# A weight ring filled by halves: two transfers for each pair of weight chunks

## The reference

```python
for l in range(2):                      # first model
    proj = rmsnorm(x) @ w_in            # 1024 x 9x1024 and more
    y = gates * (ssd(...) @ w_ssd_out, mla(...) @ w_mla_out, gdn(...) @ w_gdn_out)
    h = x + sum(y) @ w_out
    x = h + square(relu(rmsnorm(h) @ w_up)) @ w_down
x = rmsnorm(x) * final_gain
for i in range(2):                      # second model, with a context of 256 more tokens
    mods = silu(c, c_ctx) @ ada_w[i] + ada_b[i]
    x = x + g1 * mixer(modulated(x))    # neighbourhood attention, then a gated scan
    x = x + g2 * (silu(a) * u) @ ffn_w_out[i]   # a, u = modulated(x) @ ffn_w_in[i]
```

## Time and profile before

| | |
|---|---|
| Median of 3 runs | 2593.07 us (2590.92 to 2595.86) |
| Span of the profiled execution, first to last instruction | 2594.1 us |
| TensorE busy | 2512.4 us (97%), 19246 matmuls |
| VectorE, ScalarE, GpSimd busy | 1460.9, 1250.7, 312.5 us |
| Moved by the weight queue | 375.90 MB, 41.6% of 16 DMA engines' time |
| Ring transfers | 1024 KB each, 4.8 us from issue to landing (median) |

### The profile page before, as it was taken

The page is one execution under the profiler, slowest core; times in us unless marked ns, Lnnn a source line. Parts: engine busy times, 40 slices in busy tenths (PEclk is TensorE's granted clock), DMA queues, the critical chain, the costliest instruction groups (busy, mean ns, idle before and its releaser), DMA issues.

```text
span 2594.1 us, 44101 instructions
## 1 busy us (share of the span) xinstructions
PE 2512.4 (97%) x19246; PEld 2321.4 (89%) x19246; DVE 1460.9 (56%) x2242; ACT 1250.7 (48%) x1838; POOL 312.5 (12%) x179
## 2 busy tenths in 40 slices
PE   7999999999999999999999999999999999998999
PEld 7989998999999999979999886787779998888999
DVE  4773775665457557746665248553334554676554
ACT  6645554454366365445554267542223443335442
POOL 5113000000151120000000005200000001331000
PEclk9999999999999999999999999999999999999999
DMA  4344444455543443435554335233334542113454
GB/s 171 133 143 161 147 149 145 171 185 182 181 147 131 146 159 134 166 128 195 179 189 142 108 116 210 82 116 144 130 130 173 201 162 95 68 50 130 163 189 169
DMA packets 56018, 383.90 MB, mean 148 GB/s; under 512 B 6033, under 2 KB 9745, under 8 KB 10001
## 3 DMA queue, kind: packets, MB, share of 16 engines
q1 hardware_dynamic: 55104, 375.90, 41.6%
q10 hardware_dynamic: 720, 5.18, 0.5%
HBM read 380.01 MB, written 1.05 MB: 147 GB/s over the span
## 4 chain that ended last, share of the span: by engine, by line
PE 82%; DVE 9%; ACT 5%; DMA 2%; issue 1%; POOL 0%; DVEq 0%; POOLq 0%; ACTq 0%
PE ps L915 21%; PE ps L916 20%; PE ps L917 20%; DVE r L2112 3%; PE ps L1042 1%; PE ps L1420 1%; ACT r L1478 1%; PE ps L874 1%; PE ps L994 1%; PE ps L996 1%; PE ps L995 1%; PE ps L840 1%; PE ps L1367 1%; PE ps L953 1%; PE ps L955 1%
## 5 line engine op out<-in xcount | busy, mean ns | idle before, releaser
L915 PE MATMUL ps<-r,r 128*128 128x256 f32 (+1 forms) x4512 | 1348.4, 299 | 21.9 <-DVE r L2112 16.4
L916 PE MATMUL ps<-r,r 128*128 128x256 f32 (+1 forms) x4512 | 1333.4, 296 | 0.0
L917 PE MATMUL ps<-r,r 128*128 128x256 f32 (+1 forms) x4512 | 1332.0, 295 | 0.0
L2112 DVE TENSOR_TENSOR r<-ring,r 128x1024 fp32r<-128x1024 f32 (+2 forms) x558 | 678.6, 1250 | 557.6 <-ACT r L1478 557.4
L915 PEld LDWEIGHTS ps<-r,r 128*128 128x128 f32 x4512 | 854.0, 189 | 56.4 <-issue 20.3
L917 PEld LDWEIGHTS ps<-r,r 128*128 128x128 f32 x4512 | 853.6, 189 | 24.9
L916 PEld LDWEIGHTS ps<-r,r 128*128 128x128 f32 x4512 | 854.2, 189 | 24.1 <-issue 0.5
L1478 ACT ACTIVATE r<-ring 128x1024 fp32r<-128x1024 f32 (+1 forms) x614 | 612.5, 1038 | 314.7 <-DMA ring<-in_fi 67.0
L3010 POOL TENSOR_TENSOR slab<-slab 128x512 f32<-128x512 f32 (+1 forms) x20 | 28.6, 1430 | 1300.5 <-ACT slab L1598 1280.2
L2959 POOL TENSOR_TENSOR r<-ring,r 128x1024 fp32r<-128x1024 f32 x56 | 132.7, 2390 | 231.6 <-ACT r L1478 221.7
L2203 DVE SCALAR_TENSOR_TENSOR slab<-ps,v,slab 128x255 f32<-128x255 f32 (+1 forms) x168 | 67.7, 473 | 91.1 <-ACT slab L1550 91.1
(11 more groups left out here) (332 smaller groups left out, 2771.0 us busy)
## 6 DMA issues: line engine op xcount, KB each, us to landing
ring<-in_win SPq DMA_DIRECT2D x76, 1024.0 KB, 4.8
ring<-in_ada SPq DMA_DIRECT2D x48, 1024.0 KB, 4.9
ring<-in_fi SPq DMA_DIRECT2D x44, 1024.0 KB, 4.8
ring<-in_fo SPq DMA_DIRECT2D x36, 1024.0 KB, 4.8
ring<-in_wup SPq DMA_DIRECT2D x32, 1024.0 KB, 4.8
ring<-in_wdn SPq DMA_DIRECT2D x32, 1024.0 KB, 4.8
ring<-in_hin SPq DMA_DIRECT2D x20, 1024.0 KB, 4.8
ring<-in_nqkv SPq DMA_DIRECT2D x12, 1024.0 KB, 4.8
```

The source lines that it names most:

```text
L915: self.mm(o, hi[:, k - k0, cs], xh, k == 0, False)
L916: self.mm(o, hi[:, k - k0, cs], xl, False, False)
L917: i = self.mm(o, lo[:, k - k0, cs], xh, False, k == last)
L2112: self.tt(K.low(p), K.raw(p), K.high(p).bitcast(F32), ALU.subtract).then_inc(*self.up("w_lo_v", p))
```

## The change

Each chunk gets a transfer of its own. A half of a ring slot is free when its own last chunk is used up, so SyncE waits for that chunk and not for the last one of the unit. There are six semaphores in place of three, one for each half. `rings` notes for each chunk its number in its half (`raw_turn`) and the chunk that held the half before (`raw_before`).

```diff
@@ rings
         self.hi_of, self.hi_before, self.by_pool, at, split = {}, {}, {}, {}, {}
+        self.raw_turn, self.raw_before, filled = {}, {}, {}
         for p, (mat, _, c) in enumerate(self.plan()):
+            half = self.raw_at(p) // SLOT
+            before = filled.setdefault(half, [])
+            self.raw_turn[p], self.raw_before[p] = len(before) + 1, before[-1] if before else None
+            before.append(p)
             if mat == "ada":
                 continue
@@ raw_sem, raw_value
-        return self.sem(f"raw{self.unit_of[p] % RAW}")
+        return self.sem(f"raw{self.raw_at(p) // SLOT}")
-        return 16 * (self.unit_of[p] // RAW + 1)
+        return 16 * self.raw_turn[p]
@@ SyncE.program
         for u, chunks in enumerate(K.pairs):
-            if u >= RAW:
-                e.wait_ge(*K.at("dense_p", ("chunk", K.pairs[u - RAW][-1])))
...
             src = K.d[mat][layer, c // 2]
-            at = 2 * (u % RAW) * SLOT
-            e.dma_start(K.ring[:, at:at + src.shape[1]], src).then_inc(K.raw_sem(chunks[0]), 16)
+            for i, p in enumerate(chunks):
+                if K.raw_before[p] is not None:
+                    e.wait_ge(*K.at("dense_p", ("chunk", K.raw_before[p])))
+                at, n = K.raw_at(p), src.shape[1] // len(chunks)
+                e.dma_start(K.ring[:, at:at + n], src[:, i * n:i * n + n]).then_inc(K.raw_sem(p), 16)
```

## The result

The changed kernel takes **2600.7 us** (median of 15 runs, 2596.29 to 2606.41); the kernel before took 2594.76 beside it (15 runs, 2590.43 to 2600.89). The ratio is 1.0026, with a 95% interval of 1.0019 to 1.0033: 6 to 7 us slower, where 5.5 us less was forecast. So the traces can account for 3.3 us, and the rest has to come from the timed runs. By its time of 2595.86, and not its span of 2594.1, the profiled execution of before stands 2.8 us above the median of the first three runs, not 1.0; the forecast of the difference does not hang on that, only its absolute 2587.6.

A forecast was written before the change was run, and what follows sets the result against it. TensorE, busy 97%, was taken as the bound. Idle time -3.9, clock -1.7 and added costs +0.1 us sum to -5.5, so 2587.6 us from the median 2593.07; eight-in-ten range 2583.0 to 2592.5.

The forecast's parts named there:

- What it adds: Costs of more issues, waits and the later start: nothing for SyncE and ScalarE, 0 taken for TensorE, 0.1 us in all.
- more than the chain shows: Rival: ScalarE's and VectorE's earlier splits and a second low clock stretch give another 1.7 to 3.4 us, about 2585; chance 0.15.
- 708.25: TensorE's idle 1.76 us at layer 1's first unit: gain 1.7 us, or 1.0 with a half landing in 4.8 us.
- The clock term: TensorE's lowered clock after 708: 3.4 us at the lower level, not 6.8, winning 1.7 us of work; bounds 0 and 3.4.
- 1726.78: TensorE's idle 0.80 us behind one late split of a first half: the whole 0.80 goes.
- the 0.4 before L840: One TensorE idle time behind the transfer of 2201.26, a first half's split late: gain 0.4 us.
- 2368.91: TensorE's idle 1.73 us behind two splits: gain 0.9 us, with 0.8 staying because VectorE writes x until 2366.91.
- The last place: At 2379.39, TensorE's L1009 waiting for squares behind x additions: gain 0.1 us taken, bounds 0 and 1.9.
- Landing of a half: A 512 KB ring transfer lands 3.6 us after its issue, bounds 2.4 and 4.8, against 4.82 for a whole.
- The start: Constants behind one more issue delay GpSimd's first split: 0.1 us taken, bounds 0 and 0.7, as bytes set the time.
- SyncE's issues "so nothing": SyncE issues 710 ring transfers for 356, 0.33 us each, but mostly stands waiting: no cost.
- the rival of short rows: Rival: 4096 B rows costing at least 0.83 of 8192 B ones slow the DMA queues: 2600 to 2640 us; chance 0.03.

The follow-up runs named there:

- e2: Changed kernel, with GpSimd's split of chunk 10 in each layer held until VectorE's chain of small operations is done: 2591.8 us, ratio 0.9980.
- e1: Changed kernel, each unit still two transfers with own signals, but both waiting for the slot's last chunk: 2596.17 us, ratio 1.0000 to the kernel before.
- e3: Changed kernel, with GpSimd splitting only chunks 0 to 3 of each layer's input projection: 2591.26 us, ratio 0.9976 to the kernel before.
- e7: Kernel before, with GpSimd's split of chunk 10 held until VectorE's chain of small operations is done: 2593.96 us, ratio 0.9996.
- e5: Changed kernel, with vectors and constants asked for behind the first half transfer, ahead of the second: 2601.19 us, ratio 1.0024 to the kernel before.
- e8: Kernel before, each unit moved as two transfers begun when the whole slot is free, one signal for both: 2600.72 us, ratio 1.0024.
- e10: e8 with GpSimd splitting only chunks 0 to 3 of each layer's input projection: 2599.69 us, ratio 1.0019 to the kernel before.
- e4: Kernel before, with GpSimd splitting only chunks 0 to 3 of each layer's input projection: 2594.81 us, ratio 0.9997.

## Why the prediction was wrong

**The step that failed** stands under "What it adds": every cost was sought in issues, waits and landings, and engines off the path came out at "nothing". That ScalarE and VectorE "have their splits ready earlier" appears as a gain alone, in the rival "more than the chain shows". None of the rivals on the slow side was a collision. What the runs showed in its place: idle time of TensorE of 4.51 and 1.26 us and a low stretch of the clock behind each, 6.3 + 3.0 = 9.3 us in the trace, 12 us by e2.

The trace of before could have told it. It held the blocked operation at 746.03, and a pause of 1.48 us of GpSimd over the chain at 50.7, and ScalarE's split that ended that pause had itself waited 1.56 us for a transfer (50.98, shown with e1), just what the change removes. I read TensorE's waits and the engines that end them, but did not ask of an idle time of another engine who was working in it.

**The predicted gains, one by one.** At 708.25 the idle time fell from 1.76 to 0.58, not to 0 (its timeline, and the clock in the stretches of the earlier trace rows; the changed kernel lags by 3.6 us ahead of this place and 2.4 behind it):

```profile
710.65 1.13 PE L1014 MATMUL ps<-slab,cst 128*128 128x256 f32 x4 [0.58 <-ACT slab L1603]
...
704.00:712.00 8.00, 7.20 (x62) 5.76 (x60) 1.11 (x2) 4.22 (x5) 4.76 (x2) 1.00 0.65 201
712.00:720.00 8.00, 5.71 (x35) 5.71 (x36) 6.11 (x16) 5.29 (x12) 0.24 (x1) 0.79 0.04 14
```

Both halves landed 4.6 us after their issue there (700.15 and 702.99), not 3.6, each beside one that was still under way, and ScalarE's table load began at 708.67.

**The clock term** was mis-sized. The low time came out as forecast, 0.21 x 8 x 2 = 3.4 us for 6.8, but its worth of 1.7 us did not. The forecast counted all 6.8 us of before as work at half speed. TensorE worked in only 4.71 of them, since part of its idle time of 2.51 us lies inside:

```profile
709.80:716.60 6.80, 4.71 (x22) 4.71 (x23) 5.86 (x16) 4.09 (x11) 0.26 (x1) 0.50 0.02 5
```

The 3.4 us of after lie all in work, so the gain is (4.7 - 3.4) / 2 = 0.6 us. And TensorE, earlier by that, then runs into the next cover, a split of GpSimd's that did not hold it up before, with 0.41 us of new idle time:

```profile
722.20 0.38 PE L920 MATMUL ps<-r,r 128*128 128x256 f32 x1 [0.41 <-POOL r L2964]
```

The lag, 2.4 us behind 708.25, is still 2.3 at 722.98. In e2 TensorE had the full clock until that point and waited 1.80 us there. That the low time was 3.4 us is in part luck, too. In e3 the idle time is 0.64 us, nearly that of after, and the low time is 0.10 x 8 x 2 + 0.33 x 8 x 2 = 6.9 us; in e7 the idle time is 1.69, nearly that of before, and the low time is 3.4 us (two rows of e3, then one of e7, whose row before has 1.00):

```profile
704.00:712.00 8.00, 4.86 (x40) 3.42 (x40) 2.77 (x7) 4.68 (x7) 3.98 (x2) 0.90 0.45 150
712.00:720.00 8.00, 8.00 (x49) 8.00 (x49) 4.46 (x13) 4.52 (x9) 2.83 (x2) 0.67 0.01 2
```

```profile
712.00:720.00 8.00, 6.41 (x41) 6.41 (x42) 6.12 (x16) 5.26 (x11) 0.93 (x1) 0.79 0.01 3
```

So the low stretch does not simply follow the first idle time.

**The other places.** The 0.80 of 1726.78 is gone, and so is the 0.4 before L840. At 2368.91:

```profile
2374.02 1.99 PE L1047 MATMUL ps<-slab,cst 128*128 128x256 f32 x8 [0.87 <-ACT slab L1690]
```

0.87 for 1.73, where 0.8 was to stay. The last place gave 0.12 (1.25 for 1.37) for 0.1. With the 1.2 of 708.25 that is 1.2 + 0.8 + 0.4 + 0.9 + 0.1 = 3.4 us of the 3.9 of idle time.

**Landing of a half**: 3.6 us for in_win, as estimated, but 4.4 for in_ada, still within the bounds.

**The start** was taken at 0.1 and is at its bound of 0.7: 17.49 for L958, and before's 16.80 (the earlier trace rows and GpSimd's 11.99 above). "Bytes set the time, not issues" was wrong: with the same bytes ahead of them the constants were issued at 3.40 for 2.63 and landed at 11.92 for 11.22. e5 takes it back, but with one issue less and half the bytes ahead of them (issued at 2.62, landed at 10.76), so it does not tell the two apart. In the whole time it is not seen.

**SyncE's issues "so nothing"** is not contradicted by the changed kernel, where each half has its own signal; waited for together, the second issue's 0.37 us is part of what costs 6 us (e8, e10). DMA engines are busy for 45.6% instead of 41.6% with the same bytes, which the forecast named as a sign of being wrong. It is not what decided: a row of 4096 B took 159 ns where one of 8192 B took 309 (medians), 0.51 of it and far from the 0.83 at which the rival of short rows sets in, and e3, with the same rows, is faster than e4.

**The range and the chances**: the slow side got 0.06, all of it for row costs and waits of TensorE. The mechanism that decided, an engine off the path that gets no pause, had no case and no price, and its price of 9 us exceeds the whole gain.

What stays open: in how many executions of e1 the block at 60 occurs, as its ratio (1.0000) does not show the 5.6 us of its trace; why e2 recovers 12 us where the trace accounts for 9; and which low stretches of the clock belong to the change. That VectorE's operations, and not some other effect of GpSimd's splits, cost the time rests on the timelines; e2 and e3 only move or remove the splits.

## What to carry to other kernels

A transfer that lands earlier also moves the work of engines off the critical path. Before pricing it, list what those engines collide with: for each pause that the change closes, look who else worked in it, and for short operations on the path look at the longest instruction that can stand beside them. And if a unit of work is cut into two transfers, give each its own signal, or leave it whole; put constants that gate the start ahead of the second piece (0.9 us at the start, not seen in the whole time). When a lowered clock is priced, count only the part of the low stretch in which TensorE works, and look for the next wait behind it.

## What the hardware showed

- An operation of VectorE of 0.2 us (two SBUF operands, and also TENSOR_SCALAR with one) took 2.3 to 2.4 us beside a row of GpSimd splits from SBUF of 2.35 us each. One operation got through per split, so the price counts operations, not their size, and a chain of tiny ones is the worst case. With one operand in PSUM (L2208) there was no effect.
- Two transfers of 512 KB begun together complete 0.4 to 0.6 us later than one of 1 MB, which cost some 6 us over the program when both had to be there. A half of in_win in the changed kernel, mostly 2.8 us or more behind the one before, lands in 3.6 us (median), for 4.8 of a whole unit.
- Of a low stretch of the clock of 6.8 us only the 4.71 us in which TensorE worked cost time. When it shrank to 3.4 us, 0.6 us was won, and a new wait of 0.41 us took most of that.
- Nearly the same idle time (5.8 and 5.5 us) sits mostly in layer 0 or in layer 1, depending on a shift of the start by 0.9 us (4.51 and 1.26, against 1.47 and 4.02).
